# Feed forward on Trainium2: gate and up tiles multiply one 512-wide operand of hi and lo parts instead of two 256-wide ones

## The reference, cut to what matters

```
def second_block(x, p, norm_g, ffn1_wi, ffn1_wo, ...):
    h = x
    for i in range(DEPTH):                                   # DEPTH = 2
        h = h + 0.5 * swiglu(rms_norm(h, norm_g[i, 0]), ffn1_wi[i], ffn1_wo[i])
        ...
        h = h + 0.5 * swiglu(rms_norm(h, norm_g[i, 2]), ffn2_wi[i], ffn2_wo[i])
        ...
```

## Time and profile before

| what | value |
|---|---|
| median of 3 runs | 4960.62 us (4950.62 to 4961.08) |
| the profiled execution, its own time | 4963.01 us |
| its span, first to last instruction | 4961.2 us |
| TensorE busy with matmuls | 4416.8 us, 89% |
| VectorE busy | 3532.9 us, 71% |
| ScalarE busy | 2226.4 us, 45% |
| mean granted TensorE clock | 0.947 of full |

### The profile page before, as it was taken

One profiled execution on the slowest core, in us unless ns is written; L12 is line 12 of the kernel. 1 busy time (PEld: TensorE's weight loads), 2 busy tenths in 40 slices (PEclk: granted clock), 3 DMA queues, 4 the chain that ended last, 5 costly groups with the idle time before them and its releaser, 6 DMA issues. The chain is left out here.

```text
span 4961.2 us, 89574 instructions
## 1 busy us (share of the span) xinstructions
PE 4416.8 (89%) x34982; PEld 4228.4 (85%) x34982; DVE 3532.9 (71%) x6156; ACT 2226.4 (45%) x3695; POOL 1165.7 (23%) x1013
## 2 busy tenths in 40 slices
PE   6778999999899999976699999969988898988898
PEld 4567999999899999964699999959878898987798
DVE  5866987688698778746688768856675666647566
ACT  4144544444444445422354444434464444436344
POOL 0000159454016845301003954510000000000000
PEclk8889999999999999987899999989989999999999
DMA  6314876788487678732477678845414454541453
GB/s 222 126 66 151 259 233 213 263 296 284 156 259 232 215 269 299 246 127 83 149 236 253 215 240 298 297 135 187 162 47 149 152 173 163 172 148 52 137 186 131
DMA packets 293530, 952.64 MB, mean 192 GB/s; under 512 B 32640, under 2 KB 84928, under 8 KB 292342
## 3 DMA queue, kind: packets, MB, share of 16 engines
q1 hardware_dynamic: 255142, 809.08, 49.0%
q0 software_dynamic: 37248, 134.38, 8.1%
q10 hardware_dynamic: 720, 3.44, 0.2%
HBM read 900.98 MB, written 45.65 MB: 191 GB/s over the span
## 5 line engine op out<-in xcount | busy, mean ns | idle before, releaser
L153 DVE TENSOR_TENSOR weight_lo<-weight_ring,weight_hi 128x1024 fp32r<-128x1024 f32 x1356 | 1707.6, 1259 | 918.6 <-ACT weight_hi L148 900.6
L148 ACT ACTIVATE weight_hi<-weight_ring 128x1024 fp32r<-128x1024 f32 x1356 | 1428.5, 1054 | 1485.4 <-issue 775.1
L185 PE MATMUL peer01e_dot<-peer_xh,weight_hi 128*128 128x224 f32 (+1 forms) x1152 | 325.2, 282 | 9.4 <-DVE weight_lo L153 5.6
L185 PE MATMUL peer10e_dot<-peer_xh,weight_hi 128*128 128x224 f32 (+1 forms) x1152 | 324.2, 281 | 9.8 <-DVE weight_lo L153 5.6
L185 PE MATMUL peer00e_dot<-peer_xh,weight_hi 128*128 128x224 f32 (+1 forms) x1152 | 325.2, 282 | 8.6 <-DVE weight_lo L153 5.7
L185 PE MATMUL peer00e_dot<-peer_xl,weight_hi 128*128 128x224 f32 (+1 forms) x1152 | 318.0, 276 | 0.0
L185 PE MATMUL peer00e_dot<-peer_xh,weight_lo 128*128 128x224 f32 (+1 forms) x1152 | 318.0, 276 | 0.0
L185 PE MATMUL peer01e_dot<-peer_xh,weight_lo 128*128 128x224 f32 (+1 forms) x1152 | 318.0, 276 | 0.0
L185 PE MATMUL peer01e_dot<-peer_xl,weight_hi 128*128 128x224 f32 (+1 forms) x1152 | 317.9, 276 | 0.0
L185 PE MATMUL peer10e_dot<-peer_xl,weight_hi 128*128 128x224 f32 (+1 forms) x1152 | 317.1, 275 | 0.0
L185 PE MATMUL peer10e_dot<-peer_xh,weight_lo 128*128 128x224 f32 (+1 forms) x1152 | 317.1, 275 | 0.0
(11 more groups left out here) (702 smaller groups left out, 14733.5 us busy)
## 6 DMA issues: line engine op xcount, KB each, us to landing
weight_ring<-in_peer_tiles SPq DMA_DIRECT2D x768, 512.0 KB
weight_ring<-in_w_tiles SPq DMA_DIRECT2D x588, 512.0 KB
peer_acts<-peer00e_gelu SPq DMA_DIRECT2D x64, 224.0 KB
peer00e_act_in<-peer_acts SPq DMA_DIRECT2D x64, 224.0 KB
peer_acts<-peer01e_gelu SPq DMA_DIRECT2D x64, 224.0 KB
peer01e_act_in<-peer_acts SPq DMA_DIRECT2D x64, 224.0 KB
peer_acts<-peer10e_gelu SPq DMA_DIRECT2D x64, 224.0 KB
peer10e_act_in<-peer_acts SPq DMA_DIRECT2D x64, 224.0 KB
```

The costliest lines, as they stand in the source:

```text
L148: act.activation(self.tile_of(self.hi, g), self.ring[:, g % RING, :], ACT.Copy).then_inc(self.hi_done, 2)
L153: dve.tensor_tensor(self.tile_of(self.lo, g), self.ring[:, g % RING, :], self.tile_of(self.hi, g).bitcast(F32), ALU.subtract).then_inc(sel ...
L185: last = pe.matmul(out, lhsT, rhs, start=start and i == 0, stop=stop and i == len(passes) - 1, **more)
```

## The change

The hi and lo parts of the tokens now lie side by side in one tensor, `[P, KD, 2, T]`, so that for one block of 128 rows they form a row of 512 columns. For a gate or up block TensorE issues two matmuls instead of three: hi weights by all 512 columns into a full PSUM bank (the hi part's sum in the first 256 columns, the lo part's in the last 256), and lo weights by the 256 hi columns. The two halves must then be added. ScalarE copies the second half to SBUF (`copy_other`, into `other`), and VectorE adds the first half to it. The product of the up sums with `rstd` now stands ahead of the wait for SiLU. Down tiles and all other stages keep their matmuls.

```
+        other = S.sb("other", [P, 2, 2, T])
@@ TensorE, gate and up tiles
-                            last = run_passes(pe, gu[:, c % 2, j, 0:T], W.stationary(part, i * P, x(n)), n == 0, n == KD - 1)
+                            w_hi, w_lo = (w[:, part % PARTS, i * P:(i + 1) * P] for w in (W.hi, W.lo))
+                            pe.matmul(gu[:, c % 2, j, :], w_hi, x[:, n, :, :].rearrange("p a t -> p (a t)"),
+                                      start=n == 0, stop=False, skip_group_check=True)
+                            last = pe.matmul(gu[:, c % 2, j, 0:T], w_lo, x[:, n, 0, :], start=False, stop=n == KD - 1,
+                                             skip_group_check=True)
@@ ScalarE
+            def copy_other(kind, c, done):
+                act.wait_ge(W.used, end[kind, c])
+                if c >= 2:
+                    act.wait_ge(hidden, c - 1)
+                j = ("gate", "up").index(kind)
+                act.activation(other[:, c % 2, j, :], gu[:, c % 2, j, T:2 * T], ACT.Copy).then_inc(done, 1)
...
+                if kind == "gate":
+                    copy_other(kind, c, other_gate)
+                if kind == "up":
+                    copy_other(kind, c, other_up)
                 for part in (end[kind, c] - 2, end[kind, c] - 1):
                     W.next_hi(act, part)
@@ VectorE, gate
                 dve.wait_ge(W.used, end["gate", c])
+                dve.wait_ge(other_gate, c + 1)
+                chain(dve.tensor_tensor(other[:, c % 2, 0, :], gu[:, c % 2, 0, 0:T], other[:, c % 2, 0, :], ALU.add))
                 if c >= 2:
                     dve.wait_ge(silu_done, c - 1)
-                dve.tensor_tensor(scaled[:, c % 2, :], gu[:, c % 2, 0, 0:T], rstd, ALU.mult).then_inc(gated, 1)
+                dve.tensor_tensor(scaled[:, c % 2, :], other[:, c % 2, 0, :], rstd, ALU.mult).then_inc(gated, 1)
@@ VectorE, up
                     dve.wait_ge(W.used, end[kind, c])
+                    dve.wait_ge(other_up, c + 1)
+                    chain(dve.tensor_tensor(other[:, c % 2, 1, :], gu[:, c % 2, 1, 0:T], other[:, c % 2, 1, :], ALU.add))
+                    chain.mark(dve.tensor_tensor(hid[:, :], other[:, c % 2, 1, :], rstd, ALU.mult))
                     dve.wait_ge(silu_done, c + 1)
-                    chain(dve.tensor_tensor(hid[:, :], silu[:, c % 2, :], gu[:, c % 2, 1, 0:T], ALU.mult))
-                    chain(dve.tensor_tensor(hid[:, :], hid[:, :], rstd, ALU.mult))
+                    chain.wait()
+                    chain(dve.tensor_tensor(hid[:, :], silu[:, c % 2, :], hid[:, :], ALU.mult))
@@ the callers: one tensor for both parts
-        x_hi, x_lo = sb("x_hi", [P, KD, T], F32R), sb("x_lo", [P, KD, T], F32R)
+        x_both = sb("x", [P, KD, 2, T], F32R)
+        x_hi, x_lo = x_both[:, :, 0, :], x_both[:, :, 1, :]
```

More of the change, by code:

```diff
@@ L1033, in feed_forward @@
         hid_lo = S.sb("hid_lo", [P, 2, T], F32R)
-        gated, silu_done, hidden, ordered, pair_done, h_done, prompt_in, prompt_high = (
-            S.sem(n) for n in ("gated", "silu_done", "hidden", "ordered", "pair_done", "h_done", "prompt_in", "prompt_high"))
+        other_gate, other_up, gated, silu_done, hidden, ordered, pair_done, h_done, prompt_in, prompt_high = (
+            S.sem(n) for n in ("other_gate", "other_up", "gated", "silu_done", "hidden", "ordered", "pair_done", "h_done", "prompt_in", "prompt_high"))
         rstd = stats.rstd[:, 0:T]
@@ L2487, in second_layer @@
         in_rstd = sb("in_rstd", [P, T + 2])
-        x_hi, x_lo = sb("x_hi", [P, KD, T], F32R), sb("x_lo", [P, KD, T], F32R)
+        x_both = sb("x", [P, KD, 2, T], F32R)
+        x_hi, x_lo = x_both[:, :, 0, :], x_both[:, :, 1, :]
         x = split_pair(x_hi, x_lo)
-        feed_forward(nc, W, "ffn1_" + n, split_pair(*x_in), h, Statistics(h, ones, rstd), h_split((x_hi, x_lo), layer, 1))
+        in_pair = x_in[:, :, 0, :], x_in[:, :, 1, :]
+        feed_forward(nc, W, "ffn1_" + n, x_in, h, Statistics(h, ones, rstd), h_split((x_hi, x_lo), layer, 1))
         merged = sb("merged", [P, KD, T])
-        m_hi, m_lo = x_in
+        m_hi, m_lo = in_pair
         with ExitStack() as inner:
@@ L2607, in second_layer @@
         p_hi, p_lo = sb("p_hi", [P, 2, T], F32R), sb("p_lo", [P, 2, T], F32R)
-        feed_forward(nc, W, "ffn2_" + n, x, h, Statistics(h, ones, rstd), h_split((x_hi, x_lo), layer, 3),
+        feed_forward(nc, W, "ffn2_" + n, x_both, h, Statistics(h, ones, rstd), h_split((x_hi, x_lo), layer, 3),
                      prompt=(p_in, p_hi, p_lo, dram["p" + n]))
@@ L2621, in second_layer @@
                  stats=Statistics(h, ones, rstd), stats_after=KD - 1, stats_first=KD,
-                 follow=Prompt(merged, pw, h, h_split(x_in, 1, 0) if layer == 0 else None))
+                 follow=Prompt(merged, pw, h, h_split(in_pair, 1, 0) if layer == 0 else None))
 def store_stage(nc, y, out):
@@ L2675, in build @@
             high = nc.sbuf_usable_end // 32 * 32 - 2 * 4 * KD * T
-            x_in = [nc.alloc_sbuf_tensor_at("layer_in_" + part, [P, KD, T], F32R, offset=high + i * 4 * KD * T)
-                    for i, part in enumerate(("hi", "lo"))]
+            x_in = nc.alloc_sbuf_tensor_at("layer_in", [P, KD, 2, T], F32R, offset=high)
             at_in = col_at("norms")
-            scale_split(nc, "first_split", h, x_in, lambda c: cols2[:, at_in + c:at_in + c + 1])
+            scale_split(nc, "first_split", h, (x_in[:, :, 0, :], x_in[:, :, 1, :]), lambda c: cols2[:, at_in + c:at_in + c + 1])
             for layer in range(2):
```

## The result

The changed kernel takes 4969.35 us in the median (4965.03 to 4977.98), the kernel before 4960.07 us (4948.14 to 4965.73) in runs taken beside it. The ratio is 1.0021, with a 95% interval of 1.0014 to 1.0028. So it is slower by 7 to 14 us, where +1 us was forecast. The profiled execution took 4970.04 us, its span is 4968.2 us and its mean clock 0.945.

What follows compares the result with a forecast made beforehand. TensorE's pace was taken as the bound, VectorE's chain at two ends. First feed forward +0.5 - 2.5 + 1.4 = -0.6 us, second +0.5 - 0.8 + 1.4 + 0.1 = +1.2; two each +1.2, giving 4961.8 us; range 4951 to 4975.

Steps and rivals of the forecast that it cites:

- the ring: VectorE and ScalarE's cycle per chunk, growing 7.10 to 8.27 us, hidden; as slower rival it becomes the bound, 4974, chance 0.21.
- a wide pass without a gain: Rival in gate and up blocks: two passes cost as much as three now; +8 us, 4969, chance 0.10.
- What bounds the kernel: Inside a feed forward TensorE's own pace; VectorE's chain only ahead of the first and last down tiles.
- What the change takes off TensorE: Gate and up tiles shorten by 0.063 us in first, 0.020 in second feed forwards; 7.3 us over 176 tiles.
- The two rows that were added up: Gate and up block priced as one 512-wide plus one 256-wide matmul: 344.0 ns first, 351.5 ns second feed forwards.
- The rule of the Trainium skill's page: Weight loads overlap matmuls only on other array rows; 1408 loads less would give 150 us, which the trace contradicts.
- The eleven steps: VectorE and ScalarE's operations in one chunk, read to 0.01 us each, whose sum gave 8.27 us.
- the ring rival: VectorE's down-tile rests from chunk 2 on become the bound, from 8.34 us a chunk; slower, 4974, chance 0.21.
- The side input's split: Extra work in a second feed forward, costing the VectorE and ScalarE cycle 1.1 us once; counted as 0.1 us.
- The first down tile: TensorE's wait ahead of it, 1.83 us, grows by about 0.5 us to about 2.5.
- The last down tile: TensorE's wait ahead of it, 1.61 us, grows by 1.44 to about 3.1 from copies and adds in VectorE's chain.
- the sum at the two ends: Longer waits ahead of first and last down tiles cost +0.5 and +1.4 us a feed forward.

Runs made afterwards that it cites:

- no_adds: Changed kernel with the copies and adds left out, so the second half of each sum is never read; 4959.92 us, ratio 0.9990.
- filled: Changed kernel plus unread matmuls on TensorE, 18 in the wait ahead of the first down tile and 24 ahead of the last; 4967.71 us, ratio 1.0013.
- three_passes: Changed kernel with three 256-column passes a block instead of the 512-column one, copies and adds kept; 4982.94 us, ratio 1.0036.
- before_hid_first: Kernel before, with the last up tile's four hid steps moved ahead of VectorE's weight rest for the next stage; 4965.03 us, ratio 0.9997.
- ends_old: Changed kernel with chunks 0 and 21 of each feed forward put back to the old form; 4959.53 us, ratio 0.9994.
- ends_new: Kernel before, with the change only in chunks 0 and 21 of each feed forward; 4976.21 us, ratio 1.0028.
- copy_later: Changed kernel with ScalarE's copy placed behind the weight split instead of ahead of it; 4970.12 us, ratio 1.0015.
- ends_old_tail: ends_old with the last up tile's hid steps ahead of the weight rest, and the last rest behind the h steps; 4959.21 us, ratio 0.9994.

## Why the prediction came out as it did

The time is inside the range and the sign of the change, slower at the edge of what can be measured, had a chance of 0.21. The number itself, +1.2 us, was missed by 8 us. That the time is inside the range is luck: its upper part was drawn for the ring and for a wide pass without a gain, and what filled it was a cost that the forecast did not have. Step by step:

- **What bounds the kernel.** Right. TensorE's own pace sets the middle, in all kernels with a wide pass alike (8.40 and 8.49 us a chunk, with or without copies and adds); VectorE's chain sets the two ends.
- **What the change takes off TensorE.** The mechanism was right, the size was about 70% of the forecast. The 512-wide pass and the 256-wide one in turn take 348 ns a block, not 344, and 353, not 351.5; the gate and up tiles gain 5.2 us (no_adds) where the sum had 7.3. The two rows that were added up stand for runs of passes of one width. The forecast also read the pace of before a little too fast, from one chunk of 8.47 us where the average is 8.49. The rule of the Trainium skill's page "TensorE: Matmul & The Clock Gate", section "The mechanism", from which 150 us had been worked out as an estimate, does not hold here: in no_adds 1408 loads less give 5 us. The same section also lets a load into the background weight buffer run ahead of the matmuls in flight; no run here shows whether these loads do that.
- **The ring.** It was forecast at 8.27 us and is 8.35. The eleven steps were right but for one: from the `rstd` product (L1148) to the `silu` product (L1151) it takes 0.53 us, not 0.45. That product waits both for the step before it and for ScalarE's SiLU. Why that costs 0.08 us more is not shown. TensorE's chunk came out 0.06 longer than forecast as well, so a margin of 0.05 us stayed, and the ring rival did not come true. The side input's split, forecast at 0.1 us a second feed forward, cost nothing in the first layer and 0.3 us in the second (two chunks of 8.72 and 8.58 us).
- **The first down tile.** Forecast as a wait of about 2.5 us and a cost of 0.5; the row says 2.24, which is 0.4 more. Right in the main, though 1.83 and 0.5 make 2.3 and not 2.5.
- **The last down tile.** Forecast +1.44 and 3.1 us; measured +1.53 and 3.14. Right.
- **The step that failed** is the sum at the two ends. It priced a longer wait as the wait alone. The down tile behind it was taken at the earlier trace rows's pace of 118.3 ns a matmul, and that held only as long as the clock did. Behind waits of 2.24 and 3.14 us the granted clock fell to its lower level for most of the tile, in six of the eight cases: +4.1 and +5.1 us. `filled`, which changes nothing but TensorE's idleness, takes 9.0 of these 9.2 us off the tiles; the pauses behind grow by 1.6, so that 7.2 us come back in all. Nothing in the prediction asked what the clock does behind a wait that grows, although the pause ahead of the next stage already ends at the lower level in the kernel before (its matmuls of 0.55 us above).

The clock, with the rest, explains the sum: waits +8.0, down tiles at the ends +9.2, everything else up to the last wait -5.2, pauses -1.3, together +10.7.

Two rivals were near it. That the wide pass gains nothing would have given 4969, the number that was measured, by another mechanism: three_passes shows that without any gain the kernel would stand at 1.0036. And the chance of 0.21 for slower was given to the ring, which was not the cause.

What stays open is when the clock falls. At the first down tile it fell behind 1.76 us in one of four cases of before_hid_first, behind 1.89 us in one of four of ends_old (whose first chunk is that of before), behind 2.18 us in one of four of ends_new, and behind 2.21 to 2.24 us in three of four of the changed kernel; in the kernel before, with 1.76 to 1.83 us, in none of four. In the second feed forward of the second layer it did not fall in any of these kernels at the first down tile (2.25 us of wait and a tile of 2.92 us in the changed kernel). Of the last down tiles behind 2.59 us and more that of the first layer's second feed forward was spared in the changed kernel and in copy_later, and none in ends_new and three_passes. So the same wait is followed by a fall in one case and by none in another, and no run here shows what tells them apart. Since one fall is worth 1.2 to 2.4 us, a kernel's sum from its one trace holds this chance as well.

Also open is whether any version beats the kernel before. ends_old and its two variants have 0.9994 each, with intervals that include 1 (0.9985 to 1.0003 at the widest); their traces show 4 to 7 us less in the feed forwards, which is less than a measurement of this kernel can tell.

## What to carry to other kernels

A gain per tile is worth its count of tiles, and a step added to a chain is worth the number of places where the chain is exposed; here a margin of 1.37 us hid the steps in 80 chunks, and eight exposed places turned a gain of 5 us into a loss of 10. When a change lengthens a wait of TensorE, price the matmuls behind the wait at both clock levels, not only the wait. And apply such a change only where the cover is: the first and last item of a pipelined loop can keep their old form, as in ends_old, which took the loss away but was not shown to beat the kernel before.

## What the runs showed of the hardware

- In the changed kernel, 24 matmuls of 256 columns took 4.1 to 5.5 us behind a wait of 2.2 to 3.2 us where the clock fell, against 2.9 to 3.1 us at the full level. In the first feed forward it fell 1.3 us after the work of the first down tile had started again (3325.95 to 3327.23), and in the last down tile the full level was back 3.2 us after its start (3501.70 to 3504.88). Matmuls whose result nobody reads, put into the wait, kept the clock at 1.00 in all eight cases of filled.
- A weight load costs next to nothing here behind matmuls of 256 columns: taking one of three away, with its columns kept, shortens a block by about 6 ns with `layer_in` (chunks of 8.49 and 8.40 us, over 16 blocks) and by about 2 ns with `second_x` (8.52 and 8.49).
- Two weight rests of VectorE in a row take 2.36 us, 1.13 apart. An operation that waits for its own engine's last result and for another engine's as well (L1151) started 0.53 us behind that last one instead of 0.45.
- TensorE's first matmul of the next stage starts 0.80 to 0.82 us behind VectorE's last instruction of a feed forward, in before, before_hid_first and ends_old_tail alike.
